# Attention values with v stationary, both blocks of probabilities moving and the sums divided by channel rows, in a two-layer encoder

## The reference

```python
def rms_norm(x, g):
    xf = x.astype(jnp.float32)
    y = xf * lax.rsqrt(jnp.mean(xf * xf, axis=-1, keepdims=True) + RMS_EPS)
    return (y * g.astype(jnp.float32)).astype(x.dtype)

def fourier_mixer(h, w_in, w_out):
    u = (h @ w_in).reshape(B, S, 4, 256)
    f = jnp.fft.fft2(u.astype(jnp.float32), axes=(1, 3), norm="ortho").real
    return f.reshape(B, S, D) @ w_out

def neighbourhood_attention(h, w_qkv, rpb, w_o):      # 4 rows of 64 tokens, 16 heads of 64
    q, k, v = split(h @ w_qkv); q = q * 64 ** -0.5
    # a token sees all 4 rows and a clamped window of 16 columns, with a learned bias
    sc = jnp.einsum('bwhd,bawkhd->bhwak', q_r, k_g).astype(jnp.float32) + b_r[None]
    p = jax.nn.softmax(sc.reshape(B, N_HEADS, GRID_W, kh * WIN_W), axis=-1)
    return jnp.einsum('bhwak,bawkhd->bwhd', p, v_g) ... @ w_o

def swiglu(h, w_gate, w_up, w_down):                  # 1024 -> 2816 -> 1024
    return (jax.nn.silu(h @ w_gate) * (h @ w_up)) @ w_down

# layer 0: h += fourier_mixer(rms_norm(h)); h += swiglu(rms_norm(h))
# layer 1: h += neighbourhood_attention(rms_norm(h)); h += moe(rms_norm(h)), top 2 of 8 experts,
#          each expert a swiglu 1024 -> 3584 -> 1024, gates by softmax of the two router logits
# out = rms_norm(h, final_norm)
```

## Time and profile before

| | |
|---|---|
| runs, median of 3 | 1367.61 us (1366.85 to 1368.39) |
| profiled execution | 1367.15 us |
| its span, first to last instruction | 1365.3 us |
| around the span | 1.85 us |
| PE, PEld, DVE, ACT busy | 1344.7, 1117.9, 1111.9, 923.2 us |
| chain that ended last | PE 95%, DVE 3%, ACT 1%, issue 1% |

### The profile page before, as it was taken

How to read it: one execution, slowest core, us unless ns; L and a number is a source line. 1 busy time by engine, 2 the same in 40 slices (tenths; PEclk the granted TensorE clock), 3 DMA queues, 4 the chain that set the end, 5 groups by cost and what they waited for, 6 DMA issues and landing times.

```text
span 1365.3 us, 17406 instructions
## 1 busy us (share of the span) xinstructions
PE 1344.7 (98%) x6341; PEld 1117.9 (82%) x6341; DVE 1111.9 (81%) x815; ACT 923.2 (68%) x755; POOL 34.5 (3%) x48
## 2 busy tenths in 40 slices
PE   8999999999999999999999999999999999999997
PEld 7888888787878888888888888888888888888885
DVE  5756666655678889888988988898898889889997
ACT  6554444545647778777777877877787787777774
POOL 0000000000101000000000000000000000002000
PEclk8999999999989999999999999999999999999999
DMA  9666775563339999999999999999999999999992
GB/s 354 246 207 179 210 211 190 175 204 104 101 109 378 383 378 365 395 382 357 398 388 372 373 394 377 358 398 388 368 376 394 367 370 397 381 374 385 396 394 90
DMA packets 194971, 432.32 MB, mean 317 GB/s; under 512 B 19632, under 2 KB 22064, under 8 KB 194800
## 3 DMA queue, kind: packets, MB, share of 16 engines
q1 hardware_dynamic: 178784, 416.28, 83.4%
q0 software_dynamic: 3360, 11.78, 2.2%
q10 hardware_dynamic: 12784, 3.69, 1.8%
HBM read 425.94 MB, written 5.78 MB: 316 GB/s over the span
## 4 chain that ended last, share of the span: by engine, by line
PE 95%; DVE 3%; ACT 1%; issue 1%; DMA 0%; POOL 0%; DVEq 0%; ACTq 0%
PE bank_G L1250 10%; PE bank_G L1252 10%; PE bank_G L1251 10%; PE bank_U L1250 10%; PE bank_U L1252 10%; PE bank_U L1251 10%; PE bank_Y L1250 8%; PE bank_Y L1252 8%; PE bank_Y L1251 8%; PE bank_T L1696 2%; PE bank_T L1250 1%; PE bank_T L1252 1%; PE bank_T L1251 1%; DVE w_lo L753 1%; PE bank_G L1512 0%
## 5 line engine op out<-in xcount | busy, mean ns | idle before, releaser
L753 DVE TENSOR_TENSOR w_lo<-raw,w_hi 128x2048 fp32r<-128x2048 f32 x390 | 885.9, 2289 | 184.6 <-ACT w_hi L458 183.8
L458 ACT ACTIVATE w_hi<-raw 128x2048 fp32r<-128x2048 f32 x390 | 748.6, 1920 | 276.6 <-PE bank_U L1252 98.2
L1250 PE MATMUL bank_Y<-w_hi,hidT_hi 128*128 128x512 f32 x492 | 192.2, 391 | 0.0
L1252 PE MATMUL bank_Y<-w_hi,hidT_lo 128*128 128x512 f32 x492 | 191.6, 389 | 0.0
L1251 PE MATMUL bank_Y<-w_lo,hidT_hi 128*128 128x512 f32 x492 | 191.5, 389 | 0.0
L1250 PE MATMUL bank_U<-w_hi,xg_hi 128*128 128x512 f32 x448 | 179.1, 400 | 0.0
L1250 PE MATMUL bank_G<-w_hi,xg_hi 128*128 128x512 f32 x448 | 175.2, 391 | 1.3 <-DVE xg_lo L774 0.9
L1252 PE MATMUL bank_U<-w_hi,xg_lo 128*128 128x512 f32 x448 | 175.0, 391 | 0.0
L1251 PE MATMUL bank_U<-w_lo,xg_hi 128*128 128x512 f32 x448 | 174.5, 390 | 0.0
L1252 PE MATMUL bank_G<-w_hi,xg_lo 128*128 128x512 f32 x448 | 174.5, 390 | 0.0
L1251 PE MATMUL bank_G<-w_lo,xg_hi 128*128 128x512 f32 x448 | 174.4, 389 | 0.0
(11 more groups left out here) (301 smaller groups left out, 1363.5 us busy)
## 6 DMA issues: line engine op xcount, KB each, us to landing
raw<-in_expert_w_gate SPq DMA_DIRECT2D x112, 1024.0 KB, 7.7
raw<-in_expert_w_up SPq DMA_DIRECT2D x112, 1024.0 KB, 7.8
raw<-in_expert_w_down SPq DMA_DIRECT2D x112, 1024.0 KB, 7.7
raw<-in_nat_w_qkv SPq DMA_DIRECT2D x12, 1024.0 KB, 5.1
raw<-in_ffn_w_gate SPq DMA_DIRECT2D x11, 1024.0 KB, 8.9
raw<-in_ffn_w_up SPq DMA_DIRECT2D x11, 1024.0 KB, 5.7
raw<-in_ffn_w_down SPq DMA_DIRECT2D x11, 1024.0 KB, 5.2
raw<-in_fourier_w_out SPq DMA_DIRECT2D x4, 1024.0 KB, 15.6
```

Of the source, the lines that this page charges most:

```text
L458: nc.scalar.activation(w_hi[w][:], raw[s][:], ACT.Copy).then_inc(hi_made, 1)
L753: nc.vector.tensor_tensor(w_lo[w][:], raw[s][:], w_hi[w][:].bitcast(f32), ALU.subtract).then_inc(lo_made, 1)
L1250: nc.tensor.matmul(out_, xh, wh, start=start, stop=False)
L1252: return nc.tensor.matmul(out_, xl, wh, start=False, stop=stop)
```

## The change

The attention's values are turned round. `pair_values` multiplies with v stationary (128 x 64 per head) and the probabilities of both token blocks moving (256 columns), so that the output comes by channel: head 2p in partitions 0 to 63, head 2p + 1 in 64 to 127 of one 256-column region of a bank. Four matmuls per pair replace eight. The outputs need no transposes after that; `outputs_transposed` is gone. The division by the sums now needs the reciprocals along the columns: `pair_scales` (DVE) takes a reciprocal with 128 x 256 outputs per pair (each sum 64 times), PE transposes it in two transposes, ACT copies it to SBUF (`scale_copy`), and DVE multiplies 128 x 256 values (`scaled_values`). ACT's copies of transposed heads and its exponentials now alternate by head.

Beside it: `still(23)` for `still(12)`; the Fourier mixer uses four banks for `token_dft` and four for `channel_dft`; PE's waits on `act_lo` stand at each two tiles for streams 1 and 2; `stream_lo(2, 0)` stands ahead of the weight piece that it followed, and `stream_lo(2, 1)` behind the next one; in the last expert the last three steps of the gate weights move to step 6, the last down product runs all four tiles of the first 512 columns first and scatters them between the two halves of the other, and the results are added, squared and summed by halves of 512 columns.

```diff
@@ -186,7 +186,7 @@
-                       ("p_sum", [P, NB, HEADS], f32), ("p_inv", [P, NB, HEADS], f32)]
+                       ("p_sum", [P, NB, HEADS], f32), ("p_inv", [P, 2, NB, P], f32), ("scale", [P, 2, S], f32)]
@@ -313,12 +313,27 @@
-    OT = [U[0], Y[0], G[0], G[1]]
+    def values_of(p):
+        c0 = S * (p // 2 % 2)
+        return (U, Y)[p % 2][p // 4][:, c0:c0 + S]
+    def scales_of(p):
+        if p < PAIRS // 2:
+            return values_of(p + PAIRS // 2)
+        return (U[0], Y[0], G[0], G[1])[p - PAIRS // 2][:, :S]
+    BY_TOKEN = [T[0], T[1], G[0], G[1]]
+    BY_CHANNEL = [Y[0], Y[1], U[0], U[1]]
...
+    hn_cols = hn[:].rearrange("p b d -> p (b d)").rearrange("p (k s) -> p k s", s=S)
@@ -613,18 +629,28 @@
+        def scale_copy(p):
+            act.wait_ge(a_rT, p + 1)
+            if p >= 2:
+                act.wait_ge(a_out, p - 1)
+            nc.scalar.activation(att["scale"][:, p % 2], scales_of(p), ACT.Copy).then_inc(a_scale, 1)
         for p in range(PAIRS + 1):
             if p == PAIRS:
                 output_hi(0)
                 output_hi(1)
-            if p:
-                for g in (2 * p - 2, 2 * p - 1):
+            if p >= 3:
+                scale_copy(p - 3)
+            for half in range(2):
+                if p:
+                    g = 2 * p - 2 + half
...
                     nc.scalar.activation(att["probT"][:, g % PROBS], T[g % 2][:], ACT.Copy).then_inc(a_pTcopy, 1)
-            if p < PAIRS:
-                for i in (2 * p, 2 * p + 1):
+                if p < PAIRS:
+                    i = 2 * p + half
@@ -636,7 +662,9 @@
+        scale_copy(PAIRS - 2)
         split_past(W0)
+        scale_copy(PAIRS - 1)
         output_hi(2)
         output_hi(3)
         split_past(W0 + 1)
@@ -903,8 +936,10 @@
             last.then_inc(h_half, 1)
+            if q == 0:
+                stream_lo(2, 0)
             split_past(n - 1 + q)
-            stream_lo(2, q)
+        stream_lo(2, 1)
         split_past(n + 1)
@@ -925,22 +960,22 @@
-        def output(hg, b):
-            hs = slice(HEADS // 2 * hg, HEADS // 2 * (hg + 1))
-            if b == 0:
-                dve.wait_ge(a_exp, NB * HEADS // 2 * (hg + 1))
-                nc.vector.reciprocal(att["p_inv"][:, :, hs], att["p_sum"][:, :, hs]).then_inc(a_inv, 1)
-                dve.wait_ge(a_inv, hg + 1)
-                dve.wait_ge(a_pv, HEADS // 2 * (hg + 1))
-            last = nc.vector.tensor_tensor(hn[:, b, BANK * hg:BANK * (hg + 1)].rearrange("p (h d) -> p h d", d=HD),
-                                               OB[b][hg][:].rearrange("p (h d) -> p h d", d=HD),
-                                               att["p_inv"][:, b, hs].unsqueeze(2).to_broadcast([P, HEADS // 2, HD]), ALU.mult)
-            last.then_inc(a_out, 1)
+        def pair_scales(p):
+            dve.wait_ge(a_exp, NB * (2 * p + 2))
+            if p >= 2:
+                dve.wait_ge(a_rT, p - 1)
+            total = att["p_sum"][:, :, 2 * p:2 * p + 2].unsqueeze(3).to_broadcast([P, NB, 2, HD])
+            nc.vector.reciprocal(att["p_inv"][:, p % 2].rearrange("p b (h d) -> p b h d", h=2), total).then_inc(a_inv, 1)
+        def scaled_values(p):
+            dve.wait_ge(a_scale, p + 1)
+            nc.vector.tensor_tensor(hn_cols[:, p], values_of(p), att["scale"][:, p % 2], ALU.mult).then_inc(a_out, 1)
@@ -959,14 +994,17 @@
-            if p == PAIRS - 2:
-                output(0, 0)
-                output(0, 1)
+            if p >= 3:
+                scaled_values(p - 3)
+            if p:
+                pair_scales(p - 1)
+        scaled_values(PAIRS - 3)
+        pair_scales(PAIRS - 1)
         output_lo(0)
         output_lo(1)
         split_past(W0)
-        for b in range(NB):
-            output(1, b)
+        scaled_values(PAIRS - 2)
+        scaled_values(PAIRS - 1)
         output_lo(2)
@@ -1109,15 +1147,14 @@
         def add_result(E, e):
-            for b in range(NB):
-                dve.wait_ge(terms_added, 4 * NB)
-                for q in range(2):
+            for q in range(2):
+                for b in range(NB):
                     dve.wait_ge(e_scatter, NB * (2 * (E - LAST) + q) + b + 1)
+                    dve.wait_ge(terms_added, 4 * NB)
                     part = h[:, b, BANK * q:BANK * (q + 1)]
                     src = T[q] if b == 0 else (G, U)[q][1]
-                    last = nc.vector.scalar_tensor_tensor(out=part, in0=src[:], scalar=mo["weight"][:, b, bass.ds(e, 1)],
-                                                          in1=part, op0=ALU.mult, op1=ALU.add)
-                last.then_inc(e_added, 1)
+                    nc.vector.scalar_tensor_tensor(out=part, in0=src[:], scalar=mo["weight"][:, b, bass.ds(e, 1)],
+                                                   in1=part, op0=ALU.mult, op1=ALU.add).then_inc(e_added, 1)
@@ -1307,12 +1351,8 @@
-                if (n, b) == (0, 0):
-                    pe.wait_ge(act_lo_done, 4 * i + 2)
...
-                if (n, b) == (1, 0):
-                    pe.wait_ge(act_lo_done, 4 * i + 4)
@@ -1321,7 +1361,7 @@
-        still(12)
+        still(23)
@@ -1333,26 +1373,24 @@
-            if m >= 2:
-                pe.wait_ge(pt_lo_done, m - 1)
+            if m >= 4:
+                pe.wait_ge(pt_lo_done, m - 3)
...
-                last = three(T[m % 2][:, S * b:S * (b + 1)], fo["u_hi"][:, b, o:o + P], fo["u_lo"][:, b, o:o + P],
+                last = three(BY_TOKEN[m % 4][:, S * b:S * (b + 1)], fo["u_hi"][:, b, o:o + P], fo["u_lo"][:, b, o:o + P],
...
-            if g >= 2:
-                pe.wait_ge(ft_channels, 2 * (g - 1))
...
-                    last = three(Y[g % 2][:, S * r:S * (r + 1)].rearrange("p (b t) -> p b t", b=NB),
+                    last = three(BY_CHANNEL[g][:, S * r:S * (r + 1)].rearrange("p (b t) -> p b t", b=NB),
@@ -1479,17 +1520,10 @@
         def wo_product(c, half, b):
             pe.wait_ge(a_olo, 2 * half + 2)
+            if (c, half) == (0, 0):
+                pe.wait_ge(a_out, PAIRS - 3 + b)
@@ -1525,18 +1559,26 @@
-        def head_values(g):
-            pe.wait_ge(a_pTcopy, g + 1)
-            if g == HEADS // 2:
+        def pair_values(p):
+            pe.wait_ge(a_pTcopy, 2 * p + 2)
+            if p == 0:
                 pe.wait_ge(qkv_act, 6)
                 pe.wait_ge(qkv_dve, 6)
-            o = HD * (g % (HEADS // 2))
+            if p >= 2:
+                pe.wait_ge(a_out, p - 1)
+            for k in range(NB):
+                for half in range(2):
+                    g = 2 * p + half
+                    last = nc.tensor.matmul(values_of(p)[HD * half:HD * (half + 1)], att["v"][:, k, HD * g:HD * (g + 1)],
+                                            att["probT"][:, g % PROBS, S * k:S * (k + 1)], start=(k == 0), stop=(k == NB - 1))
+            last.then_inc(a_pv, 2)
+            pe.wait_ge(a_inv, p + 1)
+            if p >= PAIRS - 2:
+                pe.wait_ge(a_biased, HEADS)
             for b in range(NB):
-                for k in range(NB):
-                    last = nc.tensor.matmul(OB[b][g // (HEADS // 2)][:, o:o + HD], att["probT"][:, g % PROBS, S * k + P * b:S * k + P * (b + 1)],
-                                            att["v"][:, k, HD * g:HD * (g + 1)], start=(k == 0), stop=(k == NB - 1))
-            last.then_inc(a_pv, 1)
+                last = nc.tensor.transpose(scales_of(p)[:, P * b:P * (b + 1)], att["p_inv"][:, p % 2, b], ident[:])
+            last.then_inc(a_rT, 1)
@@ -1549,19 +1591,14 @@
             if p >= 2:
-                head_values(2 * p - 4)
-                head_values(2 * p - 3)
-        outputs_transposed(0)
-        head_values(HEADS - 4)
-        head_values(HEADS - 3)
+                pair_values(p - 2)
...
-        head_values(HEADS - 2)
-        head_values(HEADS - 1)
+        pair_values(PAIRS - 1)
         wo_product(0, 0, 1)
         wo_product(1, 0, 0)
-        outputs_transposed(1)
@@ -1719,6 +1756,36 @@
+            def last_columns(q, rows, first=0):
+                c = STEPS - 1
+                if first == 0:
+                    ready(AT["down", c, 0], E)
+                    pe.wait_ge(e_hidT_lo, E * STEPS + (c + 1))
+                for kk in range(first, first + rows):
+                    half, k = kk // KROW, kk % KROW
+                    j = AT["down", c, half]
+                    if q == 0 and half and k == 0:
+                        ready(j, E)
+                    wh, wl = parts(j, E, KROW)
+                    cs = slice(BANK * q, BANK * (q + 1))
+                    last = three(Y[q][:], hidT_hi[c % 2][:, P * kk:P * (kk + 1)], hidT_lo[c % 2][:, P * kk:P * (kk + 1)],
+                                 wh[:, k, cs], wl[:, k, cs], False, kk == BANK // P - 1)
+                    if q and k == KROW - 1:
+                        last.then_inc(piece_used, 1)
@@ -1750,21 +1817,19 @@
-            down(STEPS - 1, 0)
-            down(STEPS - 1, 1)
+            if kept:
+                last_columns(0, 4)
```

(22 more changed lines are left out.)

85 lines of the change are left out of this document (42 added, 43 removed).

## The result

The changed kernel takes 1378.14 us (median of 6 runs, 1376.18 to 1378.94) against 1366.90 (6 runs of before): ratio 1.0082, 95% interval 1.0070 to 1.0093. It is slower by 11.2 us. I had forecast +6.2 us, 1373.5, and the time lies 0.14 us above the range's upper end. The profiled execution took 1378.94, span 1377.1; it is the slowest of the six.

The account below looks back on a forecast made before the run. PE was taken as the bound; -2.1 + 1.6 + 1.5 + 4.8 - 0.4 + 0.8 = +6.2 us on 1367.15 gave 1373.4, with 1373.5 as forecast. Its own range was 1370.5 to 1376.5, the overall range 1366 to 1378.

Parts of the forecast that it names:

- What bounds: Whole kernel: PE is busy 1344.7 of 1365.3 us, so a term counts only through PE's work or waits.
- The begin, -2.1: Start and Fourier mixer: more still products keep the clock, four banks shorten waits; -2.1 us, bounds -0.8 and -3.0.
- Ahead of qkv, +1.6 and +1.5: Before qkv: DVE makes w_lo later, PE waits +1.6 us; clock possibly lost in that gap, +1.5 us.
- The price of a reciprocal, 1.6 us: Attention on DVE: a reciprocal with 256 outputs takes 1.6 us, at 5.6 ns per element.
- The attention's own period, 4.92 us: Attention pairs: DVE becomes the bound at 4.92 us per pair, where the period was 3.82.
- The attention up to w_o, +5.6: Attention to first w_o product: starts at 365.4 instead of 359.84 us, +5.6, with six reciprocals on the path.
- Behind it, -0.8: Behind the first w_o product: PE saves the eight output transposes, 0.8 us, leaving the attention at +4.8.
- third rival: Attention: the clock also falls in PE's gaps, two lost stretches of 2.5 us each, 1378.4 us; chance 0.15.
- The end, +0.8: Last down products and scatters: second scatter starts later, halves give back about 1.2; +0.8 us, bounds -0.5 and +2.
- The last expert, -0.4: Last expert: three links fewer in DVE's step 1 remove PE's wait at 1263.27; -0.4 us.
- The streaming reciprocal: Attention on DVE: the reciprocal streams like any other operation, attention gives -0.7, total 1366.4 us; chance 0.20.
- the second rival: Begin gains all 3.0 us, qkv's weight is not late, attention gives -0.7; sum -4.4, 1362.8 us; chance 0.07.

Follow-up runs that it names:

- the second trace: The kernel before, unedited, traced once more: 1.7 us of clock lost in the begin, w_out starts at 45.50 us.
- begin_only: The kernel before with only the new begin (23 still products, four and four banks for the Fourier mixer): 1365.48 us, ratio 0.9993.
- tail_order: The changed kernel with DVE making the outputs' two act_lo ahead of scaled_values(5) and the last pair's reciprocal: 1373.82 us.
- cheap_recip: The changed kernel with each pair's reciprocal taken of the 128x4 sums in place and spread to 128x256 by a copy: 1371.93 us.
- fill: The changed kernel with idle multiplications in PE's three long waits (ahead of qkv, pair 6's values and w_o): 1374.50 us.
- early_add: The changed kernel with DVE adding the first half's results ahead of y_lo(1) instead of behind it: 1377.77 us.

## Why the prediction was wrong, point by point

- *What bounds.* Right. Every term that cost something did so by a wait of PE or by its clock, and no new cost lies elsewhere.
- *The begin, -2.1.* Against the profiled execution right (-1.9), but by luck: that execution lost 3.4 us of clock, the second trace 1.7. With the second trace as the base the term would be 0.6 to 0.9, and begin_only measured 0.5 (0.3 us lost to 2.3 gained). A term that is a clock's loss in one trace was taken for a constant.
- *Ahead of qkv, +1.6 and +1.5.* Right in both: gap 2.99 us, clock loss 1.7; the run with the old order gave back both. That the finer waits help nothing holds only with the changed order; with the old one they are worth 0.8 us. The loss of clock can stay out at this gap (tail_order's trace), so it is a chance and not a price, as I had taken it.
- *The price of a reciprocal, 1.6 us.* Eight at 1737 ns mean. With the two small ones it is (1737 - 167) / 254 = 6.2 ns per element where I had 5.6 from a base of 14 elements. The estimate of 2.1 us from the repeat count of 8 in the Trainium skill ("VectorE: DVE Perf Modes", Walkthrough: the 8-slice pipeline in each mode) lies above the measured 1.74; six of them would also have raised the sum by 3.2 us and not by 3.5. The trace's slope was the better guide. cheap_recip shows that this alone binds the pairs.
- *The attention's own period, 4.92 us.* Right to the digit on DVE, and so was the 3.8 to 4.2 for the case without it: 3.98. PE's gaps there are released by ACT's exponentials, not by DVE's bias as I wrote; these wait for DVE's maxima.
- *The attention up to w_o, +5.6.* Failed by 1.3: it was +6.9. The count of reciprocals was right, and so was everything up to the end of pair 7, 41.9 us behind the first scores in the forecast (362.1 - 320.2) and in the trace (363.4 - 321.54). Then my sum let `scaled_values(5)` follow at once. It waits 1.35 us for ACT's copy of the scale, and I had put that wait at nothing: "ACT keeps up" and "ACT's alternating order costs nothing, since DVE is the later one" hold in the pairs, but behind pair 7 ACT is the later one. tail_order took away 2.6 us, this wait and part of the last reciprocal behind it; that reciprocal was in my sum, contrary to what the expectation of that run says. (The links that I wrote down also add up to 365.25 and not to 365.4.)
- *Behind it, -0.8.* Failed, and in the profiled execution this is the step that the miss comes from most: "Behind it PE saves the eight transposes" assumed the clock kept, and +1.4 came instead, 2.2 us off (+0.3 and 1.1 us off between the second traces). With the clock kept it would have been -1.3 (fill, 12.46 instead of 13.78), so the lost clock cost 2.8 us here. The attention's end leaves PE waits of 1.89 and 2.48 us, which my own sum implied (PE has nothing to do ahead of a w_o that is 5.6 us late), but I looked for the lost clock in the short gaps of the pairs only. It is my third rival's mechanism, at another place and at half its price. fill shows it: with the long waits filled the time is 3.6 us less, qkv's 1.6 included.
- *The end, +0.8.* Failed by 1.2. The delay of the second scatter (+2.4) was forecast (+2.0); the 1.2 us given back were 0.4. Squares by halves do not help while the first additions stand behind `y_lo(1)`, and early_add shows that moving them gives 0.3 more at best.
- *The last expert, -0.4.* -0.7 in the trace; right in sign and small.
- *Rivals.* The streaming reciprocal is out by L969, and the second rival by qkv's weight, which was late. That the clock falls was given 0.15 and should have been joined to my forecast, since the same late w_o that cost 5.6 us makes the gap. The first traces' +11.8 consists of the +6.2 forecast, of 1.3, 2.2 and 1.2 of these three steps, and of 0.9 that lies in the router, the begin and the rest, within what one trace of a kernel differs from the next. The medians' +11.2 can't be divided so.

## What to carry to other kernels

Spread a division after it, not before: take reciprocals on the compact sums and let a copy do the spreading; 0.47 us did here what 1.74 did. When a term says that PE starts a stage late by some microseconds, add the question what its clock does in that gap, and read the written order of the late engine, and of the engine that it waits for, up to the instruction that is waited for. And look whether a gain read from a trace is lost clock: then a second trace is needed before it counts.
